# A 31-tap depthwise convolution on TensorE: from split products over two output phases to plain fp32 products over four

## The reference, cut to what matters

```
h = x @ w_pw1 + b_pw1
a, g = split(h, 2);  h = a * sigmoid(g)
h = causal_depthwise_conv(h, w_dw) + b_dw      # 31 taps, each channel for itself
h = silu(layer_norm(h, ln_g, ln_b))
return h @ w_pw2
```

## Time and profile before

| | us |
|---|---|
| median of 3 runs | 2545.47 (2543.56 to 2545.69) |
| profiled execution, time | 2546.59 |
| profiled execution, span | 2544.8 |
| TensorE matmul busy | 2520.1 (99%) |
| VectorE busy | 1955.3 (77%) |
| ScalarE busy | 1200.0 (47%) |

### The profile page before, as it was taken

One profiled execution on the slowest core, in us unless ns is written; L12 is line 12 of the kernel. 1 busy time (PEld: TensorE's weight loads), 2 busy tenths in 40 slices (PEclk: granted clock), 3 DMA queues, 4 the chain that ended last, 5 costly groups with the idle time before them and its releaser, 6 DMA issues. The chain is left out here.

```text
span 2544.8 us, 41246 instructions
## 1 busy us (share of the span) xinstructions
PE 2520.1 (99%) x17241; PEld 2314.1 (91%) x17241; DVE 1955.3 (77%) x2571; ACT 1200.0 (47%) x1960; POOL 1.4 (0%) x10
## 2 busy tenths in 40 slices
PE   9999999999999999999999999999999999999999
PEld 7899999889888899998898899998898999999888
DVE  6988999577454679995784479996677979999576
ACT  6775444436233254443362245444356766444335
POOL 0000000000000000000000000000000000000000
PEclk9999999999999999999999999999999999999999
DMA  5202333324322223333233224333222203333322
GB/s 156 73 12 92 113 103 108 103 88 128 95 92 91 84 89 103 107 101 108 82 101 97 94 67 123 103 108 107 92 91 93 66 26 97 103 107 102 108 82 76
DMA packets 267054, 240.10 MB, mean 94 GB/s; under 512 B 14908, under 2 KB 212852, under 8 KB 266740
## 3 DMA queue, kind: packets, MB, share of 16 engines
q1 hardware_dynamic: 266292, 236.94, 30.2%
q10 hardware_dynamic: 576, 0.52, 0.1%
HBM read 233.21 MB, written 2.10 MB: 92 GB/s over the span
## 5 line engine op out<-in xcount | busy, mean ns | idle before, releaser
L1786 DVE TENSOR_TENSOR w_lo<-raw,w_hi 128x1024 fp32r<-128x1024 f32 x287 | 345.4, 1222 | 266.0 <-ACT w_hi L1309 265.7
L1309 ACT CAST w_hi<-raw 128x1024 fp32r<-128x1024 f32 x287 | 294.8, 1045 | 372.8 <-DMA raw<-in_ffn_w_down_dram 104.1
L879 PE MATMUL psum<-h_hi,w_lo 128*128 128x512 f32 x872 | 341.4, 392 | 0.0
L881 PE MATMUL psum<-h_hi,w_hi 128*128 128x512 f32 x872 | 339.4, 389 | 0.0
L880 PE MATMUL psum<-h_lo,w_hi 128*128 128x512 f32 x856 | 333.2, 389 | 0.0
L1024 PE MATMUL psum<-a_hi,w_lo 128*128 128x256 f32 x1088 | 280.9, 286 | 6.6 <-DVE w_lo L1786 5.1
L1024 PE MATMUL psum<-a_hi,w_hi 128*128 128x256 f32 x1088 | 277.5, 284 | 0.0
L1190 PE MATMUL psum<-h_hi,w_hi 128*128 128x256 f32 x768 | 217.3, 283 | 0.0
L1191 PE MATMUL psum<-h_hi,w_hi 128*128 128x256 f32 x768 | 217.3, 283 | 0.0
L1024 PEld LDWEIGHTS psum<-a_hi,w_lo 128*128 128x128 f32 x1088 | 209.1, 192 | 8.7 <-DVE w_lo L1786 4.6
L1024 PEld LDWEIGHTS psum<-a_hi,w_hi 128*128 128x128 f32 x1088 | 209.3, 192 | 0.3
(11 more groups left out here) (362 smaller groups left out, 6494.3 us busy)
## 6 DMA issues: line engine op xcount, KB each, us to landing
raw<-in_ffn_w_gate_dram SPq DMA_DIRECT2D x176, 256.0 KB, 3.0
raw<-in_ffn_w_up_dram SPq DMA_DIRECT2D x176, 256.0 KB, 3.3
raw<-in_ffn_w_down_dram SPq DMA_DIRECT2D x176, 256.0 KB, 3.1
raw<-in_a_w_pw_dram SPq DMA_DIRECT2D x94, 256.0 KB, 3.1
raw<-in_ple_w_gate_dram SPq DMA_DIRECT2D x64, 256.0 KB, 3.2
raw<-in_b_w_in_dram SPq DMA_DIRECT2D x64, 256.0 KB, 3.0
raw<-in_c_w_in_dram SPq DMA_DIRECT2D x48, 256.0 KB, 2.9
raw<-in_b_w_out_dram SPq DMA_DIRECT2D x32, 256.0 KB, 3.1
```

Of the source, the lines that this page charges most:

```text
L879: pe.matmul(bank(grp.g, j), st_lo, mv_hi, start=(k == 0), stop=False, skip_group_check=by_tiles(grp))
L881: done = pe.matmul(bank(grp.g, j), st_hi, mv_hi, start=False, stop=(ku == last and a == UK - 1), skip_group_check=by_tiles(grp))
L1309: act.copy(hi_u[u % RING], raw_u[u % RING]).then_inc(hi_ready, 1)
L1786: dve.tensor_tensor(lo_u[u % RING], raw_u[u % RING], hi_u[u % RING].bitcast(F32), ALU.subtract)\
```

## The change

Tiles 2 to 7 (`QUADS`) all go to TensorE, in four output phases and as plain fp32 products; tiles 0 and 1 stay on VectorE. Nothing of the convolution's input or taps is split any more. A block now has 32 rows and 128 columns (32 channels times four phases, taken out of a strip of 37 blocks of 32 columns); the moving operand is read out of `conv_x` at every fourth token. A step (`quad_tap`) is four products, one for each 32-row group of the array, each 32 rows by 128 columns of plain fp32, into four PSUM banks. 34 steps make a tile. The tiles run as seven segments: 2, 3, 4, 5, 6 whole, 7 in two token halves, where a product has 64 columns. VectorE makes the strips, two memsets and one multiplication a tile (`make_blocks`).

The results leave PSUM by 16 copies of 32 partitions a segment, which also put rows and phases in place, so the DMAs on SP's queue are gone: ScalarE makes all 16 for the first two segments, then ScalarE the eight of two banks (`move`) and VectorE the eight of the others (`move_low`). A segment waits until the copies of the one two before it are done; `centre` runs at step 20 of the fourth segment (tile 5), `conv_stats(0)` at step 22 of the last. The affine no longer waits for all taps by a wait of its own, but ScalarE's copies out of the last segment stand ahead of it, and then the SiLU table.

```diff
+PHASES = 4
+ROWS = P // PHASES
+STEPS = TAPS_A + PHASES - 1
+BLOCKS = TAPS_A + 2 * (PHASES - 1)
+QUADS = (2, 3, 4, 5, 6, 7)
+SEGMENTS = ((0, None), (1, None), (2, None), (3, None), (4, None), (5, 0), (5, 1))
+VECTOR_MOVES = 2
+CENTRE_IN, CENTRE_AT = 3, 20
+STATS_AT = 22
...
-            def phase_tap(s, n, e):
-                at = e % 2 * (CW // 2) + e // 2
-                for w, x in ((0, 1), (1, 0), (0, 0)):
-                    for r in range(2):
-                        moving = conv_split(n, x)[r * TILE_ROWS:(r + 1) * TILE_ROWS, at:at + HALF]
...
+            def quad_tap(s, i, e):
+                n, (v0, n_v) = SEGMENTS[i][0], segment_span(i)
+                for r in range(PHASES):
+                    moving = rows(by_phase(conv_x[:, QUADS[n], :]), r)[:, e % PHASES, e // PHASES + v0:e // PHASES + v0 + n_v]
+                    block = rows(tap_blocks(n), r)[:, e * ROWS:e * ROWS + P]
+                    last = pe.matmul(segment_bank(s, i, r), block, moving, start=(e == 0), stop=(e == STEPS - 1))
...
+                for i, (n, h) in enumerate(SEGMENTS):
+                    if i < 2:
+                        take_half(s.taps_g + i)
                     else:
+                        pe.wait_ge(moved_high, moved(s, i - 2))
+                        pe.wait_ge(moved_low, moved(s, i - 2))
...
+                    for e in range(STEPS):
+                        last = quad_tap(s, i, e)
+                        if i == CENTRE_IN and e == CENTRE_AT:
                             centre(s)
+                        if i == LAST and e == STATS_AT:
+                            conv_stats(s, 0)
...
+            def move(s, i):
+                act.wait_ge(taps_done, moved(s, i))
+                for y, out_of in moves(s, i, HIGH):
+                    last = act.copy(y, out_of)
+                last.then_inc(moved_high, 1)
+                if i < VECTOR_MOVES:
+                    for y, out_of in moves(s, i, LOW):
+                        last = act.copy(y, out_of)
+                    last.then_inc(moved_low, 1)
...
+            def make_blocks(s, n):
+                own.add(dve.memset(blocks[:, 0:edge], 0.0))
+                own.add(dve.memset(blocks[:, BLOCKS - edge:BLOCKS], 0.0))
+                dve.tensor_tensor(blocks[:, edge:edge + TAPS_A], many(rep[:, :], TAPS_A),
+                                  taps.broadcast_to([P, TAPS_A, ROWS]), ALU.mult).then_inc(blocks_made, 1)
...
             def conv_sums_of(s):
+                move_low(s, 2)
                 dve.wait_ge(centre_saved, c + 1)
+                dve.tensor_tensor(three(conv_tile(0, 2), 2), three(conv_tile(0, 2), 2), many(mean[:, :], 2), ALU.subtract)\
+                   .then_inc(z_ready, 1)
+                place_centred(s, 2)
                 place_centred(s, 3)
+                wait_moved(s, 2)
+                place_centred(s, 4)
...
+                dve.wait_ge(sq_ready, SQ_READY * c + 1)
+                own.add(dve.tensor_tensor(tiles(tmp, 0, 2), tiles(tmp, 0, 2), tiles(tmp, 2, 2), ALU.add))
...
+                own.add(dve.tensor_tensor(sum_sq, tiles(tmp, 0), tiles(tmp, 1), ALU.add))
+                move_low(s, 3)
+                wait_moved(s, 3)
+                place_centred(s, 5)
...
@@ block.scalar, conv_norm
+                for i in range(WHOLE, LAST):
+                    move(s, i)
+                    if i < LAST - 1 or WHOLE == LAST - 1:
+                        conv_half_square(s, i)
+                load_sqrt()
+                half_moments(s, 0)
+                half_root(s, 0)
+                move(s, LAST)
+                load_silu()
+                half_affine_pair(s, 0, 0)
...
@@ block.vector, conv_norm
+                move_half(s, 5)
+                add_half(s, 5)
+                add_half_square(s, 5)
                 half_root(s, 0)
                 half_scale(s, 0, 0)
                 half_scale(s, 0, 1)
+                move_half(s, 6)
...
                     if grp.index == 0:
                         convolve(s, 0, *w, 0, 10, TAPS_A, "a_b_dw", lo_end_at=ahead)
+                        make_blocks(s, 0)
+                        make_blocks(s, 1)
...
-                        convolve_alone(s, 2, K_SHARED, TAPS_A)
-                        phase_add(s, 2)
-                        norm_centre_sum(y)
+                        centre_sum(s)
```

More of the change, by code:

```diff
@@ L381, in tap_block @@
[L381 to L401, removed]
+        BLOCK_WORDS = BLOCKS * ROWS
@@ new lines, in segment_span, with segment_bank, moves @@
+        def segment_span(i):
+            h, n_v = SEGMENTS[i][1], SEQ // PHASES
+            return (0, n_v) if h is None else (h * n_v // 2, n_v // 2)
+        def segment_bank(s, i, r):
+            return bank(s.taps_g + i % 2, r)[:, 0:segment_span(i)[1]]
+        def moves(s, i, groups):
+            n, (v0, n_v) = SEGMENTS[i][0], segment_span(i)
+            y = by_phase(tiles(h_f32, CONV_Y + QUADS[n]))
+            return [(rows(y, r)[:, PHASES - 1 - j, v0:v0 + n_v], rows(segment_bank(s, i, r), j))
+                    for r in groups for j in range(PHASES)]
@@ L1887, in three, with wait_moved, conv_bias, conv_tile @@
                 return ap.rearrange("p (n s) -> p n s", n=n)
-            def norm_centre_sum(z):
-                own.settle()
-                own.add(dve.tensor_tensor(tiles(tmp, 4, 2), z(0, 2), z(2, 2), ALU.add))
+            def wait_moved(s, i):
+                dve.wait_ge(moved_high, moved(s, i))
+                dve.wait_ge(moved_low, moved(s, i))
+            def conv_bias(s, m):
+                return col("a_b_dw", s.layer // 3, m)
+            def conv_tile(m, n=1):
+                return tiles(h_f32, CONV_Y + m, n)
@@ new lines, in move_low, with centre_sum @@
+            def move_low(s, i):
+                dve.wait_ge(taps_done, moved(s, i))
+                for y, out_of in moves(s, i, LOW):
+                    last = dve.tensor_copy(y, out_of)
+                last.then_inc(moved_low, 1)
+            def centre_sum(s):
+                own.settle()
+                wait_moved(s, 0)
+                wait_moved(s, 1)
+                for m in range(2):
+                    own.add(dve.scalar_tensor_tensor(tiles(tmp, 4 + m), conv_tile(2 + m), conv_bias(s, 2 + m), conv_tile(m),
+                                                     ALU.add, ALU.add))
@@ L2265, in convolve @@
                             own.add(dve.scalar_tensor_tensor(y, x, w, y, ALU.mult, ALU.add))
-            def tap_alone(s, m, k, y, fresh=False):
-                x, w = conv_x[:, m, k:k + SEQ], col("a_w_dw", s.layer // 3 * TAPS_A + k, m)
-                if fresh:
-                    own.add(dve.tensor_scalar(y, x, w, None, ALU.mult))
-                else:
-                    own.add(dve.scalar_tensor_tensor(y, x, w, y, ALU.mult, ALU.add))
-            def convolve_alone(s, m, first, end):
-                sums = tiles(h_f32, CONV_Y + m), tiles(tmp, 5)
-                for k in range(first, end):
-                    own.settle(back=1)
-                    tap_alone(s, m, k, sums[(k - first) % 2], fresh=(k == first + 1))
-                own.settle()
-                own.add(dve.tensor_tensor(sums[0], sums[0], sums[1], ALU.add))
             def gated_input(s, grp):
```

424 lines of the change are left out of this document (123 added, 301 removed).

## The result

The changed kernel takes 2633.03 us (median of 4 runs, 2632.88 to 2635.18), the kernel before in the same session 2544.89 (4 runs): ratio 1.0349, with a 95% interval of 1.0331 to 1.0367. It is 3.5% slower, where the forecast was faster: 2532, in a range of 2519 to 2620.

What follows compares the result with a forecast made beforehand. TensorE's stream of taps was taken as the bound: 52.8 us of new taps for 63.4, with waits and tail, gained 6.8 us a layer, 13.6 off 2546.6, then 1.1 lower against the median: 2532 us, range 2519 to 2620.

Steps and rivals of the forecast that it cites:

- The failed step: Whole-tile taps on TensorE: four row groups overlap as two do, 0.222 us a step, 7.55 us a tile.
- Rival 2: Taps: moving operand at every fourth word read at half rate, 0.436 us a whole step, 2604 in all; chance 0.14.
- rival 1: Taps: passes start strictly in program order, 0.444 us a step, 2614 to 2638 in all; chance 0.18.
- the rivals of the slow side: Taps: program-order starts or a slow operand feed make the kernel slower than before; chance 0.32 together.
- Rival 2's second half: Taps: instruction stream limits at 0.030 us per load or matmul, 0.48 us a step, 2650; within the 0.14.
- Halves: Tile 7's two halves: 64-column steps still paced by the load, 0.222 us a step; the lower bound was 0.13.
- Ahead of the stage: cost 0: Before the first tap: VectorE's strips are hidden, cost 0; if the cover is gone, 1 to 2 us a layer.
- Copies: 0.2 us taken: Copies out of PSUM, 32 partitions x 128 columns: 0.2 us each, 3.2 us for 16, hidden behind the taps.
- the wait ahead of tile 7: Before tile 7's first half: TensorE waits 0.5 us for VectorE's copies of tile 5.
- The tail: After the last tap: TensorE idles some 3.5 us, ended by ScalarE's affine; mixer starts at 160.1 against 166.95.
- The clock behind it: After the wait at the stage's end: TensorE's clock falls, up to 3.6 us dearer in all, 2536.
- cheap halves: Tile 7's halves at 0.13 us a step: gain 10.7 us a layer, 2523 in all.

Runs made afterwards that it cites:

- experiment 2: Changed kernel with the taps' moving operand read as 128 neighbouring words instead of every fourth (wrong inputs): 2590.49 us.
- 6: Changed kernel with buffers back at their old addresses and the input of tiles 2 to 7 stored by phase, so taps read neighbouring words: 2571.38 us.
- 4: Changed kernel with the products of row groups 2 and 3 left out except in the first and last step, reads still strided: 2663.48 us.
- experiment 3: Changed kernel with the moving operand read at every second word instead of every fourth (wrong inputs): 2591.95 us.
- experiment 9: Kernel before the change, its two-phase fp32r products reading every second word instead of contiguous ones (wrong inputs): 2626.5 us.
- experiment 7: Kernel of experiment 6 with VectorE's and ScalarE's copies moved ahead of waits and squares, and the SiLU table loaded before the last copies: 2534.24 us.
- experiment 5: Kernel before the change with 32 words more behind a_lo, so h_hi and all tiles behind it stand 128 bytes higher: 2565.9 us.
- experiment 1: Changed kernel with 32 words more behind a_lo, putting h_hi, h_lo and the tiles behind them back at their old addresses: 2613.26 us.

## Why the prediction was wrong, point by point

**The failed step** is "If four groups overlap as two do, a step costs two passes, 2 x 0.109 plus a stagger of some ns, 0.222 us". The overlap was right (experiment 2: 0.226 a step); that a pass costs what its 128 columns cost, 0.109, when it reads every fourth word was not. It costs 0.229 us, two make 0.457. 170 whole steps are 77.7 us instead of 37.7: 40 us a layer, 80 of the 101 by which the forecast missed.

**Rival 2 was the mechanism**, shown by experiments 2 and 6 (contiguous reads halve the step) and 4 (two strided groups are as slow as four), with 3 and 9 for what in the step costs. The trace before had no strided read by TensorE, so the row that I took as nearest had the right number of columns and the wrong access. I gave 0.14 to the rule that spoke against the change, with a figure (half rate, 0.436 a step) 5% below what came. Rival 2's 2604 with 7.1 us for the whole steps, 1.8 for the halves and 19.8 for placement is 2633, what was measured. The range ended at 2620, inside rival 1 (to 2638), though the rivals of the slow side had 0.32 between them. By the Trainium skill (Advanced Engine Details and Errata, "Memory Cachelines") a line is 16 bytes and another line with each access is penalised: the trace agrees for the step of four words. That two hits on a line absorb the latency holds in experiment 3 (nearly) and not in experiment 9, where fp32r at two hits runs at half speed; there the measurement decides. Rival 2's second half, a limit of the instruction stream at 0.030 us each, fell: whole steps in experiment 2 issue 16 instructions in 0.226 us, 0.014 each.

**Rival 1** has the right total, 2614 to 2638, and the wrong cause; 20 us of that total are placement, and without them it would stand at 2613, just below rival 1. Its passes would start in pairs 0.11 us apart, and its step would stay at 0.444 with contiguous reads. The changed kernel's first matmuls, cut at 103.10 us, then those of experiment 2, cut at 102.10:

```profile
103.08 0.49 PE L892 MATMUL psum<-h_f,a_f 32*128 32x128 f32 x4
```

```profile
101.91 0.39 PE L892 MATMUL psum<-h_f,a_f 32*128 32x128 f32 x4
```

Four have started within 0.02 to 0.03 us, and no fifth for 0.2 us. A total that fits doesn't choose between two mechanisms with the same step.

**Halves.** I took 0.222 of a range of 0.13 to 0.222; 0.235 came, and without the stride much the same (8 x 28.9 = 0.231 us in experiment 7). Right in kind: in experiment 7 a bound other than columns holds, the load (of 128 columns as before) or the pace at which instructions come; no run here tells the two apart. 1 us a layer.

**Ahead of the stage: cost 0.** VectorE's strips were hidden as argued, but the stage starts 1.7 us late (103.08 against 101.38) by the slower 512-column products, as it does in experiment 5, where nothing but placement was changed. No step of mine asked what else a removed buffer moves. This is the second missing term, 20 us in all (experiments 1 and 5), and why the time lies beyond rival 2's 2604.

**Copies: 0.2 us taken, 0.375 measured**, just above both bounds that I named (0.37 and 0.34); these too came from contiguous rows, and written contiguously the copies take 0.256 and 0.285, within them. In the changed kernel the slow taps cover that. Without the stride it would have mattered: the wait ahead of tile 7, forecast at 0.5 us, is 3.11 in experiment 2. Of the 2.6 us more, 1.5 are the copies (3.11 against 1.6), the rest VectorE's wait for squares, which I had named and sized too small.

**The tail.** Forecast 3.5 us of idle, ended by ScalarE's affine; measured 4.45, ended by VectorE's eight copies (L1765), which I had as "no later". The clock behind it, stretches of the changed kernel:

```profile
200.00:204.00 4.00, 0.98 (x4) 0.98 (x5) 3.76 (x12) 3.94 (x9) 0.00 (x0) 0.52 0.00 0
204.00:208.00 4.00, 4.00 (x23) 3.71 (x22) 3.62 (x7) 4.00 (x10) 0.00 (x0) 0.63 0.00 0
208.00:212.00 4.00, 4.00 (x32) 3.90 (x31) 1.96 (x4) 3.09 (x8) 0.00 (x0) 1.00 0.02 4
```

As forecast from rows 9. What I did not see is that the same fall ahead of tile 7 would not be made good in 6 us but last through 24 us of half segments (experiments 2 and 6).

**The sum, corrected:** forecast -13.6; whole steps +80; halves +1.8; tail +1.9; no wait ahead of tile 7 -1; placement +19.2 (span of experiment 1 against the changed kernel's) make +88.3, against +86.4 in span. The clock behind the tail is not in this sum, and what gives back the 1.9 us and that was not traced. Two sums of the prediction were slightly off, and nothing rests on them: cheap halves give 2524, not 2523, and rival 2's instruction limit 114 us of taps and 2655, not 113 and 2650.

**Open.** Why 128 bytes of placement, up or down, cost a 512-column product 5.7 ns; no run here varied it in finer steps. Whether the stretch that counts is 16 bytes or more. What exactly lets the clock fall: waits do, and so did two of four row groups without a wait, but no run separates the groups in use from the work in them.

## What to carry to other kernels

An operand that is read with a step has another price than any contiguous row of the trace, on each engine: count the 16-byte stretches that it touches, or store it in the order in which it is read (here the write by phase made VectorE's `gated_input` longer, 1043 ns on average instead of 746, which was hidden (first tap at 100.44 us, in experiment 1 at 100.39), and took 42 us off, experiments 1 to 6). When a change drops or adds a buffer, compare the pace of a product that the change doesn't touch. After a stream is made shorter, look again for whoever was hidden behind it: here three groups of copies and one table load in another order were worth 37 us, more than the forecast gain of the whole change.

## What the runs showed of the hardware that was not expected

- 16-byte stretches: 128 of them in a matmul's moving operand take 0.229 us in plain fp32 (128 words at step four, two row groups or four) and 0.23 in fp32r (256 words at step two), twice the contiguous time. Eviction copies of 32x128 take 375 (ScalarE) and 378 ns (VectorE) written at a step of 16 bytes, 256 and 285 ns contiguous.
- Placement: moving operands 128 bytes lower or higher cost 232.3 instead of 226.6 ns for 512 columns, 20 us in a kernel of 2545.
- Four 32-row groups of plain fp32 run as rounds of four that start together, each round as long as one product's pass: 28.2 ns a matmul in experiment 2.
- The clock: after a wait of 3.1 us the granted clock stood at 0.50 for all 24.5 us of 32x64 products that followed without idle time, whereas after 4.45 us 128x256 products were back at 1.00 within 5 us of their start. With no wait ahead, the same 32x64 products kept 1.00 (experiment 7). With two of four row groups it was 0.50 from 120 to 200 us without any wait.
